# Reordering the per-head-pair pipeline of a hybrid convolution/attention layer: value transposes, logit caps, a convolution tap and late chunk copies change place

## The reference, cut to what matters

```python
h = rmsnorm(x, norm1_w)
b_g, c_g, u, q, k, v, gate_conv, gate_att = jnp.split(h @ w_in, SPLIT_POINTS, axis=-1)
cu = c_g * u                                  # gated convolution input
cu_full = jnp.concatenate([conv_prev, cu], axis=1)
conv = sum(conv_w[j] * cu_full[:, j:j + L] for j in range(3))
y_conv = (b_g * conv) @ w_proj_conv
# stick-breaking attention, 8 heads of 64, strictly causal
z = q @ k.T / 8 + bias;  log_beta = log_sigmoid(z);  log_stay = log_beta - z
log_after = cumsum(log_stay, reverse=True) - log_stay
y_att = (where(causal, exp(log_beta + log_after), 0) @ v) @ w_proj_attn
merged = sigmoid(gate_conv) * y_conv + sigmoid(gate_att) * y_att
x = x + merged @ w_out
x = x + square(relu(rmsnorm(x, norm2_w) @ w_up)) @ w_down
```

## Time and profile before

| | |
|---|---|
| median of 3 runs | 1799.13 us (1797.75 to 1799.48) |
| the profiled execution: own time, span | 1798.5 us, 1796.8 us |
| busy share of the span | PE 96%, DVE 40%, ACT 26%, POOL 25% |
| one head pair, 175 to 296 us | 121 us: PE busy 114.35, DVE 81.00, ACT 51.73, POOL 21.78 |
| mean granted clock of PE, of full speed | 0.982; 0.97 in each of the four head pairs |

### The profile page before, as it was taken

How to read it: one execution, slowest core, us unless ns; L and a number is a source line. 1 busy time by engine, 2 the same in 40 slices (tenths; PEclk the granted TensorE clock), 3 DMA queues, 4 the chain that set the end, 5 groups by cost and what they waited for, 6 DMA issues and landing times.

```text
span 1796.8 us, 28855 instructions
## 1 busy us (share of the span) xinstructions
PE 1728.2 (96%) x10936; PEld 1657.0 (92%) x10936; DVE 727.3 (40%) x1107; ACT 475.6 (26%) x890; POOL 440.5 (25%) x322
## 2 busy tenths in 40 slices
PE   5999999999999999989999999999999999999997
PEld 4888889889889888979999899999999999999997
DVE  5286593782961222136643433113311232123213
ACT  5253352552531222232233321002200220012102
POOL 4311112112121212113222233223322332233220
PEclk7999999999999999999999999999999999999999
DMA  5111101101117566734222211111111111111113
GB/s 159 43 31 36 49 24 30 55 14 53 31 37 248 163 214 216 223 126 147 73 73 80 65 47 36 47 47 47 35 47 47 47 35 47 47 47 35 47 35 111
DMA packets 171287, 134.35 MB, mean 75 GB/s; under 512 B 7854, under 2 KB 148298, under 8 KB 171210
## 3 DMA queue, kind: packets, MB, share of 16 engines
q1 hardware_dynamic: 170752, 133.20, 24.2%
q10 hardware_dynamic: 458, 0.08, 0.0%
HBM read 115.39 MB, written 17.86 MB: 74 GB/s over the span
## 4 chain that ended last, share of the span: by engine, by line
PE 88%; DVE 9%; ACT 1%; issue 1%; DMA 1%; SPq 0%; DVEq 0%; ACTq 0%
PE ps L785 77%; PE ps L897 2%; DVE sp L1445 2%; PE ps L941 2%; PE ps L907 1%; PE ps L985 1%; PE ps L953 1%; DVE tl L1455 1%; DVE zc L1447 1%; PE ps L924 1%; PE ps L923 1%; DVE bl L1525 1%; DVE yst L1606 1%; DVE br L1407 1%; DVE vhl L1467 1%
## 5 line engine op out<-in xcount | busy, mean ns | idle before, releaser
L711 POOL CAST wh<-raw 128x1024 fp32r<-128x1024 f32 x120 | 127.2, 1060 | 1285.6 <-PE ps L785 702.9
L785 PE MATMUL ps<-xh,wh 128*128 128x364 f32 (+1 forms) x960 | 333.7, 348 | 0.0
L785 PE MATMUL ps<-xl,wh 128*128 128x364 f32 (+1 forms) x960 | 318.7, 332 | 0.0
L785 PE MATMUL ps<-xh,wl 128*128 128x364 f32 (+1 forms) x960 | 318.6, 332 | 0.0
L717 POOL TENSOR_TENSOR wl<-raw,wh 128x1024 fp32r<-128x1024 f32 x120 | 296.6, 2472 | 21.6 <-POOL wh L711 21.4
L785 PE MATMUL ps<-yh,wh 128*128 128x364 f32 (+1 forms) x768 | 252.9, 329 | 0.0
L785 PE MATMUL ps<-yl,wh 128*128 128x364 f32 (+1 forms) x768 | 252.9, 329 | 0.0
L785 PE MATMUL ps<-yh,wl 128*128 128x364 f32 (+1 forms) x768 | 252.8, 329 | 0.0
L785 PE MATMUL ps<-hl,wh 128*128 128x364 f32 (+1 forms) x768 | 252.4, 329 | 0.0
L785 PE MATMUL ps<-hh,wl 128*128 128x364 f32 (+1 forms) x768 | 252.3, 329 | 0.0
L785 PE MATMUL ps<-hh,wh 128*128 128x364 f32 (+1 forms) x768 | 252.2, 328 | 0.0
(11 more groups left out here) (162 smaller groups left out, 2509.8 us busy)
## 6 DMA issues: line engine op xcount, KB each, us to landing
raw<-in_w_in SPq DMA_DIRECT2D x80, 256.0 KB, 3.6
cache<-in_cache_k SPq DMA_DIRECT2D x64, 256.0 KB, 3.7
cache<-in_cache_v SPq DMA_DIRECT2D x64, 256.0 KB, 3.6
raw<-in_w_up SPq DMA_DIRECT2D x64, 256.0 KB, 3.1
raw<-in_w_down SPq DMA_DIRECT2D x64, 256.0 KB, 3.1
gates<-gst SPq DMA_DIRECT2D x16, 544.0 KB, 5.9
gb<-gates SPq DMA_DIRECT2D x16, 544.0 KB, 5.8
xr<-in_x_prompt SPq DMA_DIRECT2D x4, 1024.0 KB, 10.6
```

The source lines that it names most:

```text
L711: g.tensor_copy(wh[s][:, :], raw[s][:, :]).then_inc(w_hi, 1)
L785: ins = mm(out, lhs[:, k * P:(k + 1) * P], rhs[:, x], start=(first and a == 0 and m == 0), stop=(last and a == n - 1 and m == 2))
```

## The change

Four edits, all in the first phase.

- `v_out 0` moves from behind dense chunk V2 to behind the slot of unit 1 (which holds `weights 0`), `v_out 2` moves behind the first dense half of the next slot.
- In every slot `cap` of the next unit moves in front of the `low` steps.
- `conv 0` (a multiplication by the tap's column) moves from DVE to ACT. The two small copies to `ends` stay on DVE.
- The convolution taps are put behind the second half of a B chunk instead of ahead of or behind the first, and DVE's copies of the late chunks stand at the next chunk's second half instead of its first.

```diff
             if has(n - 1):
                 order.append(("suffix", i, n - 1))
+            if has(n + 1):
+                order.append(("cap", i, n + 1))
             if has(n - 3):
                 order.extend(("low", i, n - 3, j) for j in range(len(groups(n - 3))))
-            if has(n + 1):
-                order.append(("cap", i, n + 1))
...
-                    if late[-1][0] == "first_half" and chunk == (B, 1):
+                    if late[-1][0] == "second_half" and chunk == (B, 1):
                         order.extend(taps)
                         taps.clear()
                     order.append(late[-1])
-                    if late[-1][0] == "first_half" and chunk == (B, 0):
+                    if late[-1][0] == "second_half" and chunk == (B, 0):
                         taps.extend(("conv", i, w) for w in range(3))
+
+            def late_work(n):
+                dense_halves(n)
+                if n == FIRST:
+                    order.append(("v_out", i, 2))
...
+            unit_slot(i, 1, nothing)
             order.append(("v_out", i, 0))
-            unit_slot(i, 1, nothing)
             dense_step()
-            order.extend([("v_out", i, 1), ("v_out", i, 2)])
+            order.append(("v_out", i, 1))
             for n in range(FIRST, upto + 1):
-                unit_slot(i, n, lambda: dense_halves(n))
+                unit_slot(i, n, lambda: late_work(n))
...
+                elif e[0] == "conv" and e[2] == 0:
+                    i = e[1]
+                    wc, outs, ins_ = taps(i, 0)
+                    chunk_read(act, i, U, 2)
+                    act.wait_ge(pad_made, i * 2 + 2)
+                    for q in range(2):
+                        A(outs[q], ins_[q], ACT.Copy, scale=wc).then_inc(conv_step, 1)
...
-                if e[0] in ("dense", "first_half"):
+                if e[0] in ("dense", "second_half"):
                     d = i * N_DENSE + 3 * e[2] + e[3]
                     if d > 0:
                         evac((d - 1) // N_DENSE, (d - 1) % N_DENSE)
```

More of the change, by code:

```diff
@@ L524, in apart, with taps @@
             eng.sem_inc(passed, 1)
+        SB = 2 + SEQ
+        def taps(i, w):
+            return (cols[:, ds(i + w * NPAIR, 1)],
+                    (br[:, ds(i * NTOK, SEQ)], br[:, ds(i * NTOK + SEQ, SMP)].rearrange("p (b t) -> p b t", t=NEW)),
+                    (vcu[:, w:w + SEQ], vcu[:, SB:NV].rearrange("p (b x) -> p b x", x=2 + NEW)[:, :, w:w + NEW]))
         def p1_over(eng):
@@ L1344, in _ @@
             v.wait_ge(cols_made, 2)
-            SB = 2 + SEQ
             def evac(i, d):
@@ L1398, in conv @@
                                    vcu[:, SB:NV].rearrange("p (b x) -> p b x", x=2 + NEW)[:, :, NEW:NEW + 2]).then_inc(ends_made, 1)
[L1399 to L1405, removed]
+                else:
+                    wc, outs, ins_ = taps(i, w)
+                    for q in range(2):
                         v.wait_ge(conv_step, i * CONV_STEPS + 1 + 2 * (w - 1) + q + 1)
-                        op = V_.scalar_tensor_tensor(out=outs[q], in0=ins_[q], scalar=wc, in1=outs[q], op0=ALU.mult, op1=ALU.add)
-                    op.then_inc(conv_step, 1)
+                        V_.scalar_tensor_tensor(out=outs[q], in0=ins_[q], scalar=wc, in1=outs[q], op0=ALU.mult,
+                                                op1=ALU.add).then_inc(conv_step, 1)
             def own_q(j):
```

## The result

| | before | after |
|---|---|---|
| median, 5 runs of each on one chip | 1799.13 us (1797.75 to 1800.78) | 1806.96 us (1804.76 to 1809.81) |
| ratio to before, 95% interval | | 1.0045 [1.0034, 1.0057] |
| profiled execution: own time, span | 1798.5, 1796.8 us | 1806.5, 1804.8 us |
| mean granted clock of the span | 0.982 | 0.982 |

The account below looks back on a forecast made before the run. PE, busy 96% of the span, was taken as the bound. Waits of 6.8 us plus 3.45 for slow clock made a pair 10.25 instead of 9.5, +3.0 us over four pairs: 1802 us, own range 1798 to 1805.

Parts of the forecast that it names:

- the waits: PE's waits in the head pairs: new ones replace the old, 6.8 us a pair against 6.5.
- The steps of edit 1 and of edits 2 to 4: Additions for each pair: PE waits 2.4 us at `turn 0 1`, about 0.1 at `av 7`, 3.3 at `av 9`, 1.0 at `av 11`.
- the tap on ACT costs nothing: First tap on ACT, ahead of `th` of unit 8: estimated 1.1 us, falling in a stretch where ACT idles 2.28 us.
- the cover of `v_out 0`: Start of a pair: POOL's split holds only `v_out 0`, ahead of DVE's idle time of some 2.8 us, so at no cost.
- the clock term: Half-clock stretches of PE behind its waits in each pair: cost 3.45 us against 3.0 before.
- I take 0.8 + 1.5 = 2.3, or 3.45 us against 3.0: Slow stretches per pair: 0.8 behind the 2.4 us wait, 1.5 behind the 3.3 us wait, 3.45 us together.
- the rival of 1806 that I gave 0.22: Three slow stretches a pair, both waits drawing 1.5: 1.8 us more a pair, 1806 us; chance 0.22.
- the 0.96 that the prediction had named as a sign of being wrong: Granted clock in the pairs: expected near 0.97; above 0.98 or under 0.96 would make the prediction wrong.
- half of 34 to 38 us less: Rival that only one new wait is missing: about 1785 us; chance 0.08 together with the full gain of 34 to 38.
- the two places of a pair: Value transposes at the pair's start and end of the B chunks: waits 2.4 and 3.3 us, added up with the rest.
- my reading in the prediction, that a single SBUF input is enough to be safe: DVE beside GpSimd: an instruction with two SBUF inputs is blocked in full, one with a single SBUF input isn't.

Follow-up runs that it names:

- e8: Kernel before with the first convolution tap on ACT at its old place and nothing else; 1800.14 us, ratio 0.9996.
- e2: Kernel before with the first tap on ACT and the taps and DVE's late copies half a chunk later, nothing else; 1814.07 us, ratio 1.0083.
- e4: Changed kernel with `v_out 2` put back directly behind `v_out 1`; 1804.91 us, ratio 1.0031.
- e11: Changed kernel with the taps and DVE's late copies back at the first halves; 1788.3 us, ratio 0.9937.
- e10: e9 with taps one each in the slots of units 9, 10, 11 and, of DVE's late copies, only B0's half a chunk later; 1768.36 us, ratio 0.9837.
- e5: e4 with DVE's splits of `v_out 1` and `v_out 2` as an own step behind `cap 3`; 1790.04 us, ratio 0.9925.
- e1: Kernel before with only `v_out 0` moved behind the slot of unit 1 and `v_out 2` behind the first half of C1; 1788.55 us, ratio 0.9961.
- e9: e8 with the value transposes behind the slot of unit 1 and DVE's splits behind `cap 3`; 1771.39 us, ratio 0.9851.

## Why the prediction was right, and where it was off

**Right: the waits.** The steps of edit 1 and of edits 2 to 4 came out as added up: `turn 0 1` 2.44 us (forecast 2.4), `av 7` 0.28 (0.1), `av 9` 3.14 (3.3), `av 11` 1.00 (1.0). The sum is 27.5 us where 27.2 was forecast. Each had the cause that was named. DVE's timeline at the B chunks, after:

```profile
265.49 0.34 DVE L1452 SCALAR_TENSOR_TENSOR zc<-ps,bias_p,diag_cap 128x128 f32<-128x128 f32 x1
...
267.20 0.43 DVE L1490 TENSOR_TENSOR br<-ps,otmp 64x256 f32<-64x256 f32 x1 [0.77 <-ACT otmp L1229]
267.66 2.87 DVE L1421 SCALAR_TENSOR_TENSOR br<-vcu,cols,br 128x1024 f32<-128x1024 f32 x4
...
272.81 0.55 DVE L1469 TENSOR_TENSOR tl<-ps,th 128x384 fp32r<-128x384 f32 x1
```

`cap 12` is done early (265.83), DVE waits 0.77 us for `otmp`, and then the 2.87 us of two taps stand ahead of `low 9`, which ends at 273.36, 0.14 before `av 9` starts.

**Right: the tap on ACT costs nothing**, though it takes longer than estimated, 1.37 us for both pieces instead of 1.1 to 1.3. ACT's timeline, after:

```profile
261.64 1.37 ACT L1201 ACTIVATE br<-vcu,cols 128x1024 f32<-128x1024 f32 x2
264.68 0.60 ACT L1220 ACTIVATE th<-ps 128x512 fp32r<-128x512 f32 x1 [1.66 <-PE ps L920]
```

ACT still has 1.66 us of idle time behind it; e8 shows no loss either.

**Off, without effect: the cover of `v_out 0`.** I had DVE idle for 2.8 us ahead of the second casts to `vhl`; it was 1.97. DVE's timeline, after:

```profile
206.24 1.56 DVE L1479 CAST vhl<-stage 128x256 fp32r<-128x256 f32 x2
...
210.56 0.50 DVE L1479 CAST vhl<-stage 128x256 fp32r<-128x256 f32 x2 [1.97 <-ACT stage L1194]
```

The first pair of casts takes 1.56 us instead of 0.50, beside POOL's split from 205.06 to 207.45. The casts have a single SBUF input and are held all the same, as the subtractions were. As forecast, what is held there stands ahead of DVE's idle time and costs nothing.

**Off: the size of the clock term.** The step "I take 0.8 + 1.5 = 2.3, or 3.45 us against 3.0" is the one that was mis-sized: the wait of 2.4 us came with one stretch instead of 0.8 and that of 3.1 with two instead of 1.5. That is three slow stretches a pair, 4.5 us instead of 3.45, in each of the four pairs. With them the sum is +1.5 a pair for the clock and +0.4 for the waits, 7.5 us in all, which is the rival of 1806 that I gave 0.22. The mechanism was that of the prediction: it is a longer half clock behind the same waits, and no new wait or transfer. Stretches counted in four pairs were too few to forecast their number from. The clock of a pair, 0.958, is a little under the 0.96 that the prediction had named as a sign of being wrong. One sum of the rivals was also wrong: half of 34 to 38 us less is about 1781, not 1785.

**What was not foreseen in the parts.** The forecast took the two places of a pair as a sum. Edit 1 alone is 10.1 us faster in its pairs, edits 1 to 3 are 10.0 faster, and edit 4 takes all of it back. What the wait of 3 us at the B chunks costs is itself and the half clock behind it: 6.8 us in each pair of the changed kernel, 3.4 or none in e2, from none to 17.1 in e4. That edit 4 draws the slow clock in the company of edits 1 to 3 is shown by e11 against the changed kernel. With edit 3 alone it isn't: the profiled executions of e8 and e2, without and with edit 4, have 41.0 and 37.6 us at half clock, and their medians are still 13.9 us apart. Why the same wait draws from none to five stretches is open.

## What to carry to other kernels

Where one engine is the bound, add up its waits and price the granted clock beside them: here 0.44 of each microsecond at half clock, and more than half of what edit 4 cost. When a block of work on a helper engine is moved to take one wait away, name the first step that now stands behind it and work out when the bound engine wants that; better cut the block up, as in e10, or move only the part that nobody waits for, as `v_split` in e5. Test the parts of a bundle alone: of the four edits here one was good (edit 1), one was neutral (edit 3), one a trade that lost 3.6 us (edit 2) and one did the harm (edit 4).

## What of the hardware was not expected

- The time at half clock isn't a property of the program. The four pairs of e4 have the same instructions and but for 0.4 us the same waits, with a granted clock of 0.96, 1.00, 0.94 and 0.93.
- It doesn't follow the sum of the waits: 41.0 us at half clock beside 23.1 us of waits in e8, 13.7 beside 21.8 in e1. The two kernels without any wait over 1.7 us in a pair had the least, 6.8 in e9 and none in e10. It goes with the length of the single wait. Every slow stretch in the pairs of the 13 kernels began between 1.2 us before and 2.3 us after the end of a wait of PE; counted by the length of that wait:

  | wait, us | waits | with a slow stretch | at half clock for each wait, mean, us |
  |---|---|---|---|
  | 3.3 to 3.9 | 20 | 20 | 6.7 |
  | 2.9 to 3.1 | 16 | 14 | 6.4 |
  | 2.4 | 12 | 10 | 3.4 |
  | 2.0 | 12 | 6 | 1.7 |
  | 1.65 to 1.8 | 12 | 6 | 2.0 |
  | 1.6 and less | 86 | 0 | 0.0 |

  Only waits from about 0.3 us on are counted, in one execution of each kernel.
- A cast on DVE from one SBUF tile into another was held beside GpSimd's split as subtractions of two SBUF tiles are (1.56 instead of 0.50 us for two). The Trainium skill, "SBUF — State Buffer", section "Who interferes with whom", says that casts can enter, when their operands meet its conditions, a mode that takes the port pair shared with GpSimd. By this the row agrees, and my reading in the prediction, that a single SBUF input is enough to be safe, left out that exception.
